# Prefetching, unit placement and issue order in a two-layer hybrid decoder step

## The reference

```python
for l in range(2):
    # shift, scale, gate of each sub-layer: silu(c) @ w_ada + b_ada, for the prompt's c and each sample's c
    h = rmsnorm(x, g_pre_mix) * (1 + scale) + shift
    if l == 0:   # retention (4 heads, chunked recurrence) beside differential attention (4 heads)
        y = concat(rmsnorm(o_ret) * silu(gate), rmsnorm(o_dif, g_diff) * (1 - lam_init)) @ w_out_ab
    else:        # gated linear attention: 4 heads, decay by log_sigmoid(a @ w_gate + b_gate) / 16
        y = (rmsnorm(o, g_gla) * silu(r)) @ w_out_c
    x = x + gate * rmsnorm(y, g_post_mix)
    h = modulate(x)                                  # second set of shift, scale, gate
    x = x + gate * rmsnorm(conv_ffn(h), g_post_ffn)  # causal width-3 convolution, gelu gate
```

## Time and profile before

| what | us |
|---|---|
| median of three runs | 3284.1 |
| profiled execution | 3288.65 |
| its span, first to last instruction | 3286.8 |
| PE busy in the span | 2991.0 |
| DVE, ACT, POOL busy | 1486.4, 1071.9, 92.7 |
| mean granted TensorE clock | 0.952 of 2.4 GHz |

### The profile page before, as it was taken

The page is one execution under the profiler, slowest core; times in us unless marked ns, Lnnn a source line. Parts: engine busy times, 40 slices in busy tenths (PEclk is TensorE's granted clock), DMA queues, the critical chain, the costliest instruction groups (busy, mean ns, idle before and its releaser), DMA issues. The chain is left out here.

```text
span 3286.8 us, 50533 instructions
## 1 busy us (share of the span) xinstructions
PE 2991.0 (91%) x19632; PEld 2743.4 (83%) x19632; DVE 1486.4 (45%) x2311; ACT 1071.9 (33%) x1988; POOL 92.7 (3%) x128
## 2 busy tenths in 40 slices
PE   6999987886999999999998989687699999999996
PEld 4899953444989999999987989476499999999995
DVE  4243135564474454444465100464555444444546
ACT  4111113345353323333334111343444323333232
POOL 0000000000000000000000000341000000000000
PEclk9999987998999999999999999798799999999998
DMA  5333177772231111111123211422332111111113
GB/s 227 136 130 108 56 256 261 277 257 76 88 107 45 45 45 47 42 45 51 38 72 136 72 60 44 182 103 80 133 128 81 39 45 51 45 45 45 44 44 113
DMA packets 144554, 320.40 MB, mean 97 GB/s; under 512 B 12481, under 2 KB 77858, under 8 KB 136114
## 3 DMA queue, kind: packets, MB, share of 16 engines
q1 hardware_dynamic: 103730, 249.68, 21.7%
q10 hardware_dynamic: 40704, 69.09, 5.9%
HBM read 273.08 MB, written 45.64 MB: 97 GB/s over the span
## 5 line engine op out<-in xcount | busy, mean ns | idle before, releaser
L250 PE MATMUL f_acc<-h_hi,f_hi 128*128 128x352 f32 x1632 | 539.0, 330 | 12.4 <-issue 6.6
L250 PE MATMUL f_acc<-h_hi,f_lo 128*128 128x352 f32 x1632 | 533.1, 327 | 0.0
L250 PE MATMUL f_acc<-h_lo,f_hi 128*128 128x352 f32 x1632 | 530.1, 325 | 0.0
L250 PE MATMUL f_acc<-m_hi,f_hi 128*128 128x352 f32 x1248 | 411.7, 330 | 4.3 <-DVE m_lo L1556 3.3
L250 PE MATMUL f_acc<-m_hi,f_lo 128*128 128x352 f32 x1248 | 406.6, 326 | 0.0
L250 PE MATMUL f_acc<-m_lo,f_hi 128*128 128x352 f32 x1248 | 404.4, 324 | 0.0
L250 PE MATMUL f_acc<-f_ghi,f_hi 128*128 128x352 f32 x1056 | 342.2, 324 | 8.5 <-DVE y L1657 8.1
L250 PE MATMUL f_acc<-f_glo,f_hi 128*128 128x352 f32 x1056 | 339.5, 322 | 0.0
L250 PE MATMUL f_acc<-f_ghi,f_lo 128*128 128x352 f32 x1056 | 339.1, 321 | 0.0
L250 PEld LDWEIGHTS f_acc<-h_hi,f_hi 128*128 128x128 f32 x1632 | 312.0, 191 | 15.5 <-issue 9.2
L1650 DVE TENSOR_TENSOR y<-y,f_acc 128x1056 f32<-128x1056 f32 x160 | 200.2, 1251 | 263.9 <-PE f_acc L250 263.9
(11 more groups left out here) (364 smaller groups left out, 4955.5 us busy)
## 6 DMA issues: line engine op xcount, KB each, us to landing
f_st<-w_ffn SPq DMA_DIRECT2D x132, 512.0 KB, 3.3
kt<-cache_k SPq DMA_DIRECT2D x128, 256.0 KB, 5.2
att_vt<-cache_v SPq DMA_DIRECT2D x128, 256.0 KB, 5.8
x<-y ACTq DMA_DIRECT2D x9, 1408.0 KB, 5.9
ret_ada_w<-w_ada ACTq DMA_DIRECT2D x12, 1024.0 KB, 5.3
y<-w_qkv SPq DMA_DIRECT2D x10, 1024.0 KB, 6.0
gla_ada_w<-w_ada SPq DMA_DIRECT2D x10, 1024.0 KB, 7.0
open_ada_w<-w_ada SPq DMA_DIRECT2D x8, 1024.0 KB, 15.2
```

The costliest lines, as they stand in the source:

```text
L250: last = nc.tensor.matmul(out, a(kk), b(kk), start=(n == 0), stop=(n == 3 * nk - 1))
```

## The change

- *Squares ahead*: in both tails ACT issues the square of job j+2 behind the root of job j.
- *Pages ahead*: in retention SP reads the page numbers at pair 1, issues the K pages behind pair 2's loads, and issues eight of the first sequence's V pages behind pair 3's loads into two tiles that now live as long as `kt`. In attention the first sequence's new values come first, then the other eight V pages. Retention's tile `svm` lies in a region of `y` now.
- *Product emptied in its step*: `take_product(s-3)` comes behind the exponentials of step s; `cached_scale` behind `take_turned`.
- *Units*: two in the gate (32, 33), fourteen in GLA (34 to 47), so two in each of the chunks 1 to 7.
- *Outputs by heads*: in GLA the outputs of the chunk before go one head at a time between scores 2 to 6, `deltas` behind the last, DVE's `state` behind select 6, ACT's `take_outputs` behind level 5.
- In the GLA samples `deltas(h)` stands ahead of the outputs of head h.

```diff
@@ stage_tail, ACT
             head_root(2)
+            head_square(4)
             head_hi(1)
             head_root(3)
+            head_square(5)
             round_unit(1)
             head_hi(2)
-            head_square(4)
             head_hi(3)
             round_unit(2)
             for j in range(4, JOBS):
                 head_root(j)
-                if j + 1 < JOBS:
-                    head_square(j + 1)
+                if j + 2 < JOBS:
+                    head_square(j + 2)
@@ stage_retention, SP, in the loop over pairs i
                     sp.dma_start(ss[:], state_in).then_inc(s_landed, 16)
-            sp.wait_ge(ids_in, 16)
-            for j, page in enumerate(load_pages(sp, ids, 0, cache_k)):
-                load_page(sp, cache_k, page, "o p h k -> p o h k", kt[j // GP], j % GP).then_inc(keys_in, 16)
+                    sp.wait_ge(ids_in, 16)
+                    page = load_pages(sp, ids, 0, cache_k)
+                if i == 2:
+                    for j in range(NPG):
+                        load_page(sp, cache_k, page[j], "o p h k -> p o h k", kt[j // GP], j % GP).then_inc(keys_in, 16)
+            for j in range(GP * len(vt)):
+                load_page(sp, cache_v, page[j], "o p f -> p o f", vt[j // GP], j % GP).then_inc(vals_in, 16)
@@ stage_attention, SP
-            values(0, load_pages(sp, ids, 0, cache_v))
+                if n < AHEAD:
+                    sp.sem_inc(cv_in[n], 16 * GP)
+            new_values(0)
+            values({j: sp.value_load(ids[0:1, bass.ds(j, 1)], min_val=0, max_val=cache_v.shape[0] - 1)
+                    for j in range(AHEAD * GP, NPG)}, AHEAD)
             with sp.Fori(1, NB) as q:
                 page = load_pages(sp, ids, q, cache_k)
                 sp.wait_ge(c_scored, q + 1)
                 for n in range(G):
                     load(n, cache_k, page, "o p h k -> p o h k", kt[n], k_in[n])
-                values(q, page)
+                new_values(q)
+                values(page, 0)
@@ stage_attention, ACT
-                for s in range(STEPS + 4):
-                    if s < STEPS and s % WIN == 3:
-                        cached_scale(i, s // WIN)
-                    if s >= 4:
-                        take_product(i, s - 4)
+                for s in range(STEPS + 3):
                     if 2 <= s < STEPS + 2:
                         for c in range(batches(s - 2)):
                             take_turned(i, s - 2, c)
+                    if s < STEPS and s % WIN == 3:
+                        cached_scale(i, s // WIN)
                     if s < STEPS:
                         exps(i, s)
+                    if s >= 3:
+                        take_product(i, s - 3)
@@ stage_gla, ACT
                 level_exp(c + 1, 4)
+                key_exps(c)
+                level_exp(c + 1, 5)
                 if c:
                     take_outputs(c - 1)
-                key_exps(c)
-                level_exp(c + 1, 5)
                 query_exps(c)
@@ stage_gla, PE
                 if c:
-                    outputs(c - 1, (0, 1))
+                    outputs(c - 1, (0,))
                 scores(c, 3)
                 if c:
-                    outputs(c - 1, (2, 3))
+                    outputs(c - 1, (1,))
                 scores(c, 4)
                 if c:
-                    deltas(c - 1)
+                    outputs(c - 1, (2,))
                 if len(ns):
                     ada.turn(pe, ns[0])
                 scores(c, 5)
+                if c:
+                    outputs(c - 1, (3,))
+                    deltas(c - 1)
                 scores(c, 6)
...
             turn_keys(NCH - 1)
+            for n in list(units(NCH - 1))[1:]:
+                ada.turn(pe, n)
@@ stage_gla, DVE
                 select(c, 4)
-                state(c - 1)
                 scale_level(c + 1, 4)
...
                 select(c, 6)
+                state(c - 1)
                 scale_queries(c)
@@ stage_gla_samples, PE
             for h in range(H):
+                if h:
+                    deltas(h)
                 for e in range(2):
...
             last.then_inc(summed, 1)
-            for i in range(1, H):
-                deltas(i)
@@ decoder_step
-            stage_gate(nc, g, a["w_a"], a["w_gate"], a["scan"], b, y_flat[:], a["w_ada"], 32, 6)
+            stage_gate(nc, g, a["w_a"], a["w_gate"], a["scan"], b, y_flat[:], a["w_ada"], 32, 2)
...
-                      [(states[:], a["state_gla"])], a["w_ada"], 38, 10)
+                      [(states[:], a["state_gla"])], a["w_ada"], 34, 14)
```

More of the change, by code:

```diff
@@ L1748, in load_page, with stage_retention @@
     return sp.dma_start(dst[:, j:j + 1], cache[bass.ds(page, 1)].rearrange(order))
-def stage_retention(nc, g, qkT, rot, val, o, state_in, state_out, sstate_out, pages, ids, cache_k, kt, w_ada):
+def stage_retention(nc, g, qkT, rot, val, o, state_in, state_out, sstate_out, pages, ids, cache_k, kt, cache_v, vt, w_ada):
     PAIRS = NCH // 2
@@ L1775, in stage_retention @@
         sv = k.sb("sv", [TS, H, DV])
-        svm = k.sb("svm", [TS, H, NB, DV])
+        svm = o[0:TS, H:2 * H, :].rearrange("p h t -> p (h t)")[:, 0:H * NB * DV].rearrange(
+            "p (h b e) -> p h b e", h=H, b=NB)
         skn = k.sb("skn", [TS, 256])
@@ L1783, in stage_retention @@
         ps_sample = ps_d[:, 1, 0:2 * H * TS].rearrange("p (a h i) -> p a h i", a=2, h=H)
-        s_landed, ids_in, keys_in, s_out = (k.sem(x) for x in ("s_landed", "ids_in", "keys_in", "s_out"))
+        s_landed, ids_in, keys_in, vals_in, s_out = (k.sem(x) for x in ("s_landed", "ids_in", "keys_in", "vals_in", "s_out"))
         s_zeroed, s_qready, s_scored, s_masked, s_ready, s_summed, s_copied, s_deltaed, s_stated = (
@@ L1824, in _ @@
             sp.wait_ge(keys_in, 16 * NPG)
+            sp.wait_ge(vals_in, 16 * GP * len(vt))
         @block.scalar
@@ L2004, in _, with stage_attention @@
             ada.finish(Seq(dve, ada_dv), 0, (2, 3, 4))
-def stage_attention(nc, g, qkT, cache_k, cache_v, ids, kt, val, o):
+def stage_attention(nc, g, qkT, cache_k, cache_v, ids, kt, v_ahead, val, o):
     SC = 64 ** -0.5
@@ L2042, in stage_attention @@
             k.sem(x) for x in ("mixed", "turned", "aready", "summed", "copied", "dv"))
-        vt = [k.sb(f"vt{n}", [P, GP, H * DV]) for n in range(G)]
+        AHEAD = len(v_ahead)
+        vt = v_ahead + [k.sb(f"vt{n}", [P, GP, H * DV]) for n in range(AHEAD, G)]
         vn = k.sb("vn", [NS, H * DV])
@@ L2091, in load, with new_values @@
                     load_page(sp, cache, page[n * GP + j], order, dst, j).then_inc(sem, 16)
-            def values(q, page):
+            def new_values(q):
                 sp.wait_ge(c_summed, q + 1)
@@ L2096, in values @@
                              bass.ds(q * NS + SEQ, NS), :].rearrange("g t f -> t g f")).then_inc(vn_in, 16)
-                for n in range(G):
+            def values(page, first):
+                for n in range(first, G):
                     load(n, cache_v, page, "o p f -> p o f", vt[n], cv_in[n])
@@ L2499, in _ @@
                 nc.scalar.activation(x[:], x[:], ACT.Ln, bias=1.0).then_inc(expd, 1)
-                for n in range(*((BETWEEN[h], BETWEEN[h + 1]) if h < 2 else (BETWEEN[2], BETWEEN[2] + 2) if h == 2
+                for n in range(*((BETWEEN[h], BETWEEN[h + 1]) if h < 2 else (BETWEEN[2], min(BETWEEN[2] + 2, n_units)) if h == 2
                                  else (BETWEEN[2] + 2, n_units))):
@@ L2880, in _ @@
                 select(c, 7)
+            for n in list(units(NCH - 1))[1:]:
+                ada.add(dve, n)
             state(NCH - 1)
@@ L3093, in decoder_step @@
             kt = [sb(first, f"kt{n}", [P, GP, H, PAGE]) for n in range(PG)]
+            vt = [sb(first, f"vt{n}", [P, GP, H * DV]) for n in range(2)]
             stage_retention(nc, g, qkT, outs["rotated"], outs["values"], y, a["state_ret"],
-                            outs["ret_prompt"], outs["ret_sample"], a["pages"], ids, a["cache_k"], kt, a["w_ada"])
-            stage_attention(nc, g, qkT, a["cache_k"], a["cache_v"], ids, kt, outs["values"], y)
+                            outs["ret_prompt"], outs["ret_sample"], a["pages"], ids, a["cache_k"], kt, a["cache_v"], vt, a["w_ada"])
+            stage_attention(nc, g, qkT, a["cache_k"], a["cache_v"], ids, kt, vt, outs["values"], y)
         recycle_semaphores(nc)
```

## The result

The changed kernel takes 3231.79 us (median of four, 3230.28 to 3233.39); one more run of the kernel before beside it brings that kernel's median to 3287.68. The ratio is 0.9831, 95% interval 0.9816 to 0.9846, so 1.7% faster. The profiled execution has a span of 3231.5 us, 55.3 less than before. A table by stages, from PE's first matmul of a stage to that of the next, shows where they came from; the terms of the forecast stand beside it.

The account below looks back on a forecast made before the run. TensorE (PE) was taken as busy almost throughout, so time is won only where it stands still or runs at the lower clock. Stage terms summed to -49.6 us, 3284.1 to 3234.5 us; range over the cases 3208 to 3262.

Parts of the forecast that it names:

- the likeliest case: Whole kernel: the forecast of 3234.5 us holds, running by itself from 3222 to 3248 us; chance 0.59.
- Squares: Both tails: sums no longer wait for ACT's square behind a root; -15.5 us in the first, -10.5 in the second.
- the clock comes back: Rival, both tails: without gaps PE keeps the upper clock level, 14.1 and 10.5 us more, 3210 us; chance 0.10.
- Pages, attention: Attention's start: no wait for V pages, second sequence's K pages issued at 514.6, PE waits 3.2 us; -9.5 us.
- I take -1: Attention, ACT's order: earlier product copy gains little against the later cached scale; -1 us, ends -16.0 and +6.8.
- the 462 to 466 of the prediction: Retention: by the skill's ring rule pair 3's keys land then, behind the pages; stage loses 0 to 2 us.
- Gate: Gate with two units: the last head's scan sets the stage's end, 2098.6 against 2102.29; -3.7 us.
- the order's -6.7: GLA's chunks, outputs by heads: one PE wait for DVE's selects goes in each of seven chunks, 0.96 us each.
- the units' +3.3: GLA's chunks: four more units cost 6.5 us uncovered; half lie in PE's remaining waits.
- The slower rival: GLA: PE waits a whole landing for a unit, 7.0 us in each of seven chunks; 3287 us, chance 0.03.
- Samples: GLA samples: second head's deltas no longer stand behind all outputs on PE; -6.5 us, ends -7 and -4.
- signs of being wrong: In the changed trace: a PE wait for weights in GLA, or the sums' wait found again before the product pieces.

## Why the prediction was right, and where its terms were not

The sum was -49.6 us to 3234.5; measured were 3231.79 us, and -55.3 in the profiles. The sign, the likeliest case and the size held, but errors of both signs stand inside. That the total came so close is in part luck: the tails gave 9.2 us more than their terms and attention 4.9 less.

- *Squares*: the mechanism was right and the size too small in both tails, 26.0 against 35.2 us. Only waiting was in the sum, and of waiting the change won less than the sum had: 12.0 us behind the first sum where 15.5 were forecast, and 8.8 where 10.5 were. Of the 27.0 and 28.9 us that were scaled, 4.1 and 10.5 lie in front of the first sum, where the stage has nothing to gain. The first piece came 4.2 us earlier (22.4 us after the first sum before, 18.2 now; forecast 4.9), but of that only 2.4 are waits (9.25 to 6.88 between the two) and 1.8 are PE's busy time. What was missing is the clock: 8.2 us of PE's busy time in the first head and 7.1 in the second. That was the rival "the clock comes back"; it came back in part, to 0.86 and 0.92, with the waits gone in part. The section "HAM oscillation — how this bites in real kernels" of the Trainium skill's "TensorE: Matmul & The Clock Gate" ties the lower clock to pauses between bursts of matmuls. Both heads agree with it; in attention the total of the pauses did not order the clocks, 39.95 us at 0.86 against 47.9 at 0.92.
- *Pages, attention*: K issued at 514.56 (514.6 forecast), PE there at 529.58 (530), waiting 3.31 (3.2); the second sequence starts 9.4 us earlier in the stage (9.5). The wait's hit to a tenth is luck: where SP's program in attention is the same, it is 2.1 to 7.0 us. Undone, the pages prove worth 12.4 us under this order, 7.6 to 13.7 with the spread of profiles.
- *Attention, ACT's order*: the step that failed. "I take -1" became +6.8 to +11.2 by the profiles (275.8 - 269.0, 263.4 - 254.9, 268.2 - 257.0; the upper end was +6.8), and +2 to +3 by the ratios of the whole times. The waits behaved as the step said: those for the copy fell from 16.0 to 3.7 us, others took their place (7.5 for the cached scale), and leaving the page waits aside (12.64 before, 3.31 after) PE stood still 41.4 us before and 36.6 now. But the same matmuls took longer, at 0.84 to 0.87 instead of 0.91 to 0.92 with the pages ahead; busy time times clock is nearly the same in both (223.45 x 0.86 = 192.2, 209.14 x 0.92 = 192.4). My ends had a price for late instructions and none for the clock. Shown is that the order of these three operations changes the granted clock and that neither move alone restores it. Which pauses let the clock fall is not shown.
- *Retention*: 85.5 us against 86.6, and 83.2 to 89.0 over all these runs: no effect to be told. Pair 3's keys did come late, and later than the 462 to 466 of the prediction: SP, busy with the pages, issued them at 458.56 instead of 452.99, and they landed 12.1 us after that instead of 4.9, at 470.61, behind the last K page (469.50). DVE waits 5.13 us; with a flight of 4.9 us they would have been in time for 465.57, when DVE was free for them. The trace agrees with the order within one ring that the Trainium skill states ("DMA: Bandwidth & Descriptors", "Queues, rings and completion order"). It doesn't prove it: a weight unit issued on ACT's queue at 458.36 also took 8.4 us, where one at 459.71 before took 4.8, and no run here separates the ring from the sharing. The stage's end does not hang on it.
- *Gate*: DVE's chain is shorter by what I took, but GLA's masks then are waited for 3.04 us, where the kernel before had 1.56, so -2.3 by PE's first matmul. The forecast ended at the scan and did not look at what stands behind it. That wait changes from profile to profile; the changed kernel's second one has 1.61.
- *GLA*: the order's -6.7 was measured as -6.0; the units' +3.3 as 0. The four more multiplies take 3.6 us, yet PE is busy 0.8 us more in the window and stands still 4.3 less (168.5 - 128.49, 165 - 129.25), at a clock of 0.90 instead of 0.88. The slower rival, a wait for a whole landing in every chunk, did not come: 1.2 us of PE's time in all. Its price, 3287, lay within the 9.9 us that the prediction itself counts as no difference.
- *Samples*: -6.5 forecast, -6.2 measured, and 41.4 us when undone; with the new order the profiles have 32.8 to 35.7.
- *Signs and chances*: the pages, retention's end, the gate, GLA's end and the second deltas came as named. Not so the sums' waits (12.5 and 13.7 us, under 12 was named), the selects (11.3, under 11 was named), and the first piece, 9.7 us behind the sums at 766.29, where 8 at most was named. Two of the signs of being wrong showed in small: 1.2 us of waiting for weights in GLA, and 2.5 and 3.7 us of waiting for DVE ahead of the first pieces. By its own parts the chance of "faster" is 0.96 (0.59 + 0.17 + 0.10 + 0.08 + 0.03 - 0.01), not 0.94.

## What to carry to other kernels

Where a stretch has pauses and a granted clock below 1, cost both: PE's busy time for the same matmuls before and after belongs in the sum beside the waits, and it can be as large. An order that removes waits can still lose, so a reordering on a helper engine is to be judged by PE's busy time as well as by its idle time. When edits touch separate stages, time by stage tells six microseconds that the whole launch's time hides. But one profile is one execution: attention as changed was profiled at 262.1 to 268.2 us, so a stage that moves by that little needs a second profile.

## What the runs showed of the hardware

- The same 1568 or 1569 matmuls of attention took 209.14 to 212.73 us at a granted clock of 0.91 to 0.93, 215.00 at 0.89 and 220.04 to 227.69 at 0.83 to 0.88. How long PE stood still in all does not sort them: 42.2 us at 0.91 and 47.9 (257.0 - 209.14) at 0.92, 39.95 at 0.86 and 48.1 at 0.88. Less idle time did not mean a higher clock.
- Sixteen page transfers of 256 KB took SP 8.92 us to issue in attention and 13.79 in retention, where modulation weights were being loaded over ACT's queue in the same stretch: the issue itself slowed, and one of the sixteen alone took 4.06 us. What slowed it was not tried.
